# Router on unnormalized rows, and output tiles finished in two halves, in a hybrid attention and MoE layer

## What is computed

```
x1    = x + ga * (mixed @ w_out)                # ga, a2, b2: one value per channel
h2    = x1 * rsqrt(mean(x1*x1) + EPS) * a2 + b2 # a2 = gain * (1 + scale), b2 = shift
score = sigmoid(h2 @ w_router)                  # 16 experts
...                                             # choose 2 experts of one group per token
out   = x1 + gm * sum over chosen experts of weight * expert(h2)
```

## Time and profile before

| | us |
|---|---|
| median of 3 runs | 2009.48 (2003.45 to 2012.72) |
| profiled execution | 2009.4 |
| its span in the trace | 2007.7 |
| output stage, first output matmul to L1408 | 1389.1 to 1504.6 |
| routing, L1408 to the first expert product | 1504.6 to 1553.8 |

### The profile page before, as it was taken

The page is one execution under the profiler, slowest core; times in us unless marked ns, Lnnn a source line. Parts: engine busy times, 40 slices in busy tenths (PEclk is TensorE's granted clock), DMA queues, the critical chain, the costliest instruction groups (busy, mean ns, idle before and its releaser), DMA issues. The chain is left out here.

```text
span 2007.7 us, 22379 instructions
## 1 busy us (share of the span) xinstructions
PE 1817.4 (91%) x8125; PEld 1254.0 (62%) x8125; DVE 933.4 (46%) x1517; ACT 664.2 (33%) x1151; POOL 364.3 (18%) x315
## 2 busy tenths in 40 slices
PE   1999999989898989989989978899983999999996
PEld 1555654555555555655656656687873888888885
DVE  5554313232333342434333436477547464648475
ACT  1421101223232333423324325434212353537373
POOL 3211140000010100101102001100001243436344
PEclk9999998999999999999989988799995999999998
DMA  9334321201110010110000010174334586979694
GB/s 340 137 126 147 85 42 34 63 30 40 37 42 26 22 37 27 29 30 22 27 21 23 15 32 1 63 265 175 126 129 164 168 298 205 305 223 381 202 360 131
DMA packets 121395, 232.38 MB, mean 116 GB/s; under 512 B 5832, under 2 KB 44816, under 8 KB 120240
## 3 DMA queue, kind: packets, MB, share of 16 engines
q1 hardware_dynamic: 113312, 203.14, 29.0%
q0 software_dynamic: 7984, 27.93, 5.7%
HBM read 196.97 MB, written 35.13 MB: 116 GB/s over the span
## 5 line engine op out<-in xcount | busy, mean ns | idle before, releaser
L1797 PE MATMUL psum<-arena 128*128 128x512 f32 x768 | 386.7, 639 | 0.5 <-ACT arena L937 0.4
L1279 DVE TENSOR_REDUCE negm<-psum 128x1 f32<-128x640 f32 (+7 forms) x128 | 90.5, 707 | 423.2 <-PE psum L1724 423.2
L1783 PE MATMUL psum<-kv,arena 128*128 128x64 f32 x1464 | 201.6, 283 | 61.9 <-DVE arena L1255 36.7
L1783 PEld LDWEIGHTS psum<-kv,arena 128*128 128x128 f32 x1464 | 192.1, 204 | 69.6 <-issue 38.2
L723 POOL TENSOR_SCALAR arena<-arena 128x128 f32<-128x128 f32 (+7 forms) x32 | 76.8, 2401 | 854.9 <-ACT arena L931 854.9
L1797 PEld LDWEIGHTS psum<-arena 128*128 128x128 f32 x768 | 144.6, 204 | 128.0 <-issue 127.7
L908 ACT ACTIVATE arena<-psum,negm 128x640 f32<-128x640 f32 (+7 forms) x128 | 89.6, 700 | 402.1 <-DVE negm L1279 402.0
L1623 PE MATMUL psum<-arena 128*128 128x512 f32 (+2 forms) x512 | 189.0, 522 | 0.0
L1921 PE MATMUL psum<-heads_r,kv_r 128*128 128x512 f32 x384 | 150.7, 393 | 15.2 <-DVE kv_r L1509 15.2
L1722 PE MATMUL psum<-kv,heads 112*128 112x512 f32 (+7 forms) x384 | 150.7, 498 | 9.2 <-ACT arena L931 8.6
L1503 DVE TENSOR_TENSOR arena_r<-arena,heads_r 128x2048 fp32r<-128x2048 f32 x64 | 146.6, 2353 | 15.1 <-ACT heads_r L994 15.1
(11 more groups left out here) (376 smaller groups left out, 2729.1 us busy)
## 6 DMA issues: line engine op xcount, KB each, us to landing
arena<-in_w_exp_gate_dram SPq DMA_DIRECT2D x16, 2048.0 KB, 12.0
arena<-in_w_exp_down_dram SPq DMA_DIRECT2D x16, 2048.0 KB, 12.5
arena<-in_w_exp_up_dram SPq DMA_DIRECT2D x16, 2048.0 KB, 14.1
arena<-in_w_ada_dram SPq DMA_DIRECT2D x7, 2048.0 KB, 15.6
arena<-in_w_in_dram SPq DMA_DIRECT2D x24, 512.0 KB, 4.0
z_dram<-arena SPq DMA_DIRECT2D x48, 256.0 KB, 2.0
arena<-z_dram SPq DMA_DIRECT2D x8, 1536.0 KB, 7.9
bc<-in_w_ada_dram SPq DMA_DIRECT2D x4, 2048.0 KB, 7.8
```

Source lines behind the costliest of these rows:

```text
L1279: dve.tensor_reduce(m1, score_buf(u)[:, 0:w], AX.X, ALU.max, negate=True).then_inc(max_ok, 1)
L1783: mm = pe.matmul(psum[:, bank, c * HD:(c + 1) * HD], pt[:, j * P:(j + 1) * P], v, start=(j == 0), stop=(j == u["nb"] - 1))
L1797: mm = pe.matmul(GATE_BANK, gate_w[t % 3][:, k, :], hT[:, k, hf * BANK:(hf + 1) * BANK], start=(k == 0), stop=(k == NK - 1))
```

## The change

The router no longer reads h2. It reads the transposed `x1`, which has neither root nor scale nor shift. The scale is multiplied into the router's weights once (`wr_a2`). The shift's part, b2 times `wr`, is a row of 16 values that 8 more products make once (`rt_bias`, on PE in pass n = 1). The root is one number per token, so DVE applies it and the shift to the 16 results of each tile (`router_logits`). For that the root of each tile gets its own column of `stp`.

`xn2` is still made, since the experts' tokens are gathered from it, but in DVE's next pass of the loop.

From tile 1 on PE finishes bank 0 (high, then low products) before bank 1, with a signal after each; in tile 0 the order is as before. DVE multiplies and adds each half when it is complete.

Thirteen semaphores of the earlier compression stage are folded into four that count; their waits stay where they are.

```diff
+            dve.wait_ge(wr_in, 32)
+            dve.tensor_tensor(wr_a2[:, :, :], wr[:, :, :], mod_a2.unsqueeze(2).to_broadcast([P, NK, NE]), ALU.mult).then_inc(wr_a2_ok, 1)
+
+            def router_logits(n):
+                dve.wait_ge(rt_full, n + 1)
+                dve.scalar_tensor_tensor(logits[:, n * NE:(n + 1) * NE], psum[:, 6 + n % 2, n * NE:(n + 1) * NE], stp[:, 1 + n:2 + n],
+                                         rt_bias[:, :], ALU.mult, ALU.add).then_inc(rt_read, 1)
+
             for n in range(NT + 1):
                 if n < NT:
-                    dve.wait_ge(out_full, n + 1)
                     dve.wait_ge(xr_in[n % 2], 16 * (n // 2 + 1))
-                    if n:
-                        dve.wait_ge(xn2_ok, n)
                     if n >= 2:
                         dve.wait_ge(x1_out[n % 2], 16 * (n // 2))
-                    t2 = x1[n % 2].rearrange("p (a d) -> p a d", a=2)
-                    own(dve.tensor_tensor(t2, psum[:, 2 * (n % 2):2 * (n % 2) + 2, :],
-                                          ga_bc[:, :].rearrange("p (a d) -> p a d", a=2), ALU.mult))
-                    dve.tensor_tensor(x1[n % 2], x1[n % 2], xr[n % 2], ALU.add).then_inc(x1_ok, 1)
+                    for h in range(2):
+                        hs = slice(h * BANK, (h + 1) * BANK)
+                        dve.wait_ge(out_full, 2 * n + h + 1)
+                        own(dve.tensor_tensor(x1[n % 2][:, hs], psum[:, 2 * (n % 2) + h, :], ga_bc[:, hs], ALU.mult))
+                        ins = dve.tensor_tensor(x1[n % 2][:, hs], x1[n % 2][:, hs], xr[n % 2][:, hs], ALU.add)
+                    ins.then_inc(x1_ok, 1)
                     if n + 2 < NT:
                         mixed_lo(n + 2)
                 if n:
+                    m = n - 1
                     dve.wait_ge(xn2T_full, n)
                     dve.tensor_copy(h2T[:, 0:4, :], psum[:, 4, :].rearrange("p (k t) -> p k t", k=4)).then_inc(h2T_dve, 1)
-                if n < NT:
-                    dve.wait_ge(x1_rstd, n + 1)
-                    if n:
-                        dve.wait_ge(xn2_out, 16 * n)
+                    dve.wait_ge(x1_rstd, n)
+                    dve.wait_ge(x1_ok, n)
+                    if m:
+                        dve.wait_ge(xn2_out, 16 * m)
                     else:
                         dve.wait_ge(mod_rows_act, 1)
-                    own(dve.scalar_tensor_tensor(xn2, x1[n % 2], stp[:, 1:2], a2_bc, ALU.mult, ALU.mult))
+                    own(dve.scalar_tensor_tensor(xn2, x1[m % 2], stp[:, 1 + m:2 + m], a2_bc, ALU.mult, ALU.mult))
                     dve.tensor_tensor(xn2, xn2, b2_bc, ALU.add).then_inc(xn2_ok, 1)
+                if n == 1:
+                    dve.wait_ge(rt_bias_full, 1)
+                    own(dve.tensor_copy(rt_bias[:, :], psum[:, 7, BANK - NE:BANK]))
+                if n >= 2:
+                    router_logits(n - 2)
+            router_logits(NT - 1)
...
             def router(n):
+                if n >= 2:
+                    pe.wait_ge(rt_read, n - 1)
                 for k in range(NK):
-                    mm = pe.matmul(psum[:, 6, n * NE:(n + 1) * NE], h2T[:, k, :], wr[:, k, :],
+                    mm = pe.matmul(psum[:, 6 + n % 2, n * NE:(n + 1) * NE], h2T[:, k, :], wr_a2[:, k, :],
...
+                    out_high(0)
+                    if n:
+                        out_low(0)
+                        out_high(1)
+                    else:
+                        out_high(1)
+                        out_low(0)
+                    out_low(1)
                 if 1 <= n <= NT:
-                    if n >= 2:
+                    if n == 1:
+                        pe.wait_ge(x1_ok, 1)
+                        for k in range(NK):
+                            mm = pe.matmul(psum[:, 7, BANK - NE:BANK], mod_b2[:, k:k + 1].to_broadcast([P, P]), wr[:, k, :],
+                                           start=(k == 0), stop=(k == NK - 1))
+                        mm.then_inc(rt_bias_full, 1)
+                        pe.wait_ge(wr_a2_ok, 1)
+                        pe.wait_ge(mod_rows_act, 1)
+                    else:
                         pe.wait_ge(h2T_act, n - 1)
                         pe.wait_ge(h2T_dve, n - 1)
                         router(n - 2)
-                    pe.wait_ge(xn2_ok, n)
+                    pe.wait_ge(x1_ok, n)
                     for k in range(NK):
-                        ins = pe.transpose(psum[:, 4 + k // 4, (k % 4) * P:(k % 4 + 1) * P], xn2[:, k * P:(k + 1) * P],
+                        ins = pe.transpose(psum[:, 4 + k // 4, (k % 4) * P:(k % 4 + 1) * P], x1[(n - 1) % 2][:, k * P:(k + 1) * P],
```

More of the change, by code:

```diff
@@ L172, in hybrid_trunk @@
             "squared", "reduced", "rstd_ok", "tok_ok", "tokT_full", "tokT_dve", "tokT_act"))
-        blk_ok, hid_full, gelu_e, gelu_in, gelu_ok, gelT_full, hid_ok, kcmp_full, kcmp_sq, kcmp_rstd, kcmp_tok, kcmpT_full, kcmp_ok = (
-            sem(s) for s in ("blk_ok", "hid_full", "gelu_e", "gelu_in", "gelu_ok", "gelT_full", "hid_ok", "kcmp_full", "kcmp_sq",
-                             "kcmp_rstd", "kcmp_tok", "kcmpT_full", "kcmp_ok"))
+        cmp_dve, cmp_act, cmp_pe, kcmp_rstd = (sem(s) for s in ("cmp_dve", "cmp_act", "cmp_pe", "kcmp_rstd"))
+        BLK, GELU_IN, GELU_OK, HID_OK, KCMP_TOK, KCMP_OK = range(1, 7)
+        GELU_E, KCMP_SQ = range(1, 3)
+        HID_FULL, GELT_FULL, KCMP_FULL, KCMPT_FULL = range(1, 5)
         mod2_ok = sem("mod2_ok")
@@ L442, in hybrid_trunk @@
         wr, rbias = sb("wr", [P, NK, NE]), sb("rbias", [P, NE])
+        wr_a2, rt_bias = sb("wr_a2", [P, NK, NE]), sb("rt_bias", [P, NE])
+        wr_a2_ok, rt_bias_full, rt_read = sem("wr_a2_ok"), sem("rt_bias_full"), sem("rt_read")
+        logits = heads[:, 6 * D:6 * D + P]
         N_BLK = 2 * T // P + NE
@@ L744, in _ @@
                 one(pool.tensor_scalar(stp[:, 0:1], st[:, SSX:SSX + 1], 1.0 / D, EPS, ALU.mult, ALU.add))
-                pool.tensor_tensor(stp[:, 1:2], stp[:, 0:1], half[:, 0:1], ALU.pow).then_inc(x1_rstd, 1)
+                pool.tensor_tensor(stp[:, 1 + n:2 + n], stp[:, 0:1], half[:, 0:1], ALU.pow).then_inc(x1_rstd, 1)
             pool.wait_ge(xn2_out, 16 * NT)
@@ L867, in _ @@
                 if cc == 2:
-                    act.wait_ge(gelu_in, 1)
-                    act.activation(tmp_ge, tmp_ge, ACT.Exp, scale=-GELU_C).then_inc(gelu_e, 1)
+                    act.wait_ge(cmp_dve, GELU_IN)
+                    act.activation(tmp_ge, tmp_ge, ACT.Exp, scale=-GELU_C).then_inc(cmp_act, 1)
                 act.wait_ge(acc_full, s + 1)
@@ L983, in _ @@
                                    ACT.Copy).then_inc(h2T_act, 1)
-            act.wait_ge(rt_full, NT)
-            act.activation(route[0], psum[:, 6, 0:P], ACT.Sigmoid).then_inc(score_ok, 1)
+            act.wait_ge(rt_read, NT)
+            act.activation(route[0], logits, ACT.Sigmoid).then_inc(score_ok, 1)
             def expert_weights_hi(e, b_e):
@@ L1004, in _ @@
             act.wait_ge(y_lo_ok, NT)
+            act.wait_ge(score_ok, 1)
             expert_weights_hi(0, None)
@@ L1200, in _ @@
             dve.wait_ge(kcmp_rstd, 1)
[L1201 to L1203 removed]
+            dve.tensor_scalar(sq[0:HD, 64:128], psum[0:HD, 2, 0:HD], stp[0:HD, 16:17], None, ALU.mult).then_inc(cmp_dve, 1)
+            dve.wait_ge(cmp_pe, KCMPT_FULL)
+            dve.tensor_scalar(kcmpT[0:HD, :], psum[0:HD, 2, 0:HD], G_KC[0:HD, :], None, ALU.mult).then_inc(cmp_dve, 1)
             own(dve.memset(sel[:, :], 0.0))
@@ L1863, in _, with out_high @@
                     pe.wait_ge(y_lo_ok, n + 1)
-                    for h in range(2):
+                    bank = [psum[:, 2 * (n % 2) + h, :] for h in range(2)]
+                    def out_high(h):
                         w = wout_hi[h].rearrange("p (k n) -> p k n", k=NK)
@@ L1868, in _, with out_low @@
                                 pe.wait_ge(wout_hi_ok, 2 * h + k // 4 + 1)
-                            pe.matmul(psum[:, 2 * (n % 2) + h, :], y_hi[n % 2][:, k, :], w[:, k, :], start=(k == 0), stop=False)
-                            pe.matmul(psum[:, 2 * (n % 2) + h, :], y_lo[n % 2][:, k, :], w[:, k, :], start=False, stop=False)
-                    for h in range(2):
+                            pe.matmul(bank[h], y_hi[n % 2][:, k, :], w[:, k, :], start=(k == 0), stop=False)
+                            pe.matmul(bank[h], y_lo[n % 2][:, k, :], w[:, k, :], start=False, stop=False)
+                    def out_low(h):
                         w = wout_lo[h].rearrange("p (k n) -> p k n", k=NK)
@@ L1875, in _ @@
                                 pe.wait_ge(wout_lo_ok, 2 * h + k // 4 + 1)
-                            mm = pe.matmul(psum[:, 2 * (n % 2) + h, :], y_hi[n % 2][:, k, :], w[:, k, :], start=False,
-                                           stop=(k == NK - 1))
-                    mm.then_inc(out_full, 1)
-                if 1 <= n <= NT:
-                    if n >= 2:
```

(7 more changed lines are left out.)

52 lines of the change are left out of this document (26 added, 26 removed).

## The result

| | before | after |
|---|---|---|
| median of 20 runs each | 2005.08 us (2002.61 to 2012.72) | 2012.18 us (2009.84 to 2020.04) |
| ratio, 95% interval | | 1.0032 (1.0021 to 1.0043) |
| profiled execution | 2009.4 us | 2013.1 us |
| its span | 2007.7 us | 2011.4 us |

The changed kernel is 0.32% slower: 6.4 us by the ratio, 4.2 to 8.6 by its interval (the ratio weighs all runs and is not the quotient of the two medians, 1.0035). That is within 0.5%, as the likeliest case had it; the forecast was +8.0 us on 2009.4, a ratio of 1.0040. More runs of the kernel before brought its median from 2009.48 down to 2005.08, so most of the distance between 2017.4 and 2012.18 lies in the base and not in the sum: on a base of 2005.08 the forecast is 2013.1.

The account below looks back on a forecast made before the run. PE bounds seven output tiles, then a chain of single steps; a 15.16 us lap through the x load exceeds PE's 13.52, moving the first routing operation from 1504.6 to 1512.6. 2009.4 + 8.0 = 2017.4 us, range 2007 to 2022.

Parts of the forecast that it names:

- the likeliest case: Whole kernel: the late x load moves the end by +8.0 us, to 2017.4; chance 0.58, its own range 2014 to 2020.
- a lap: Output stage: from one xn2 through SP, load, halves and copy to the next, 15.16 us against PE's 13.52.
- the last, without mixed_lo: Output stage, pass 6: no mixed_lo, which takes 3.30 us off and leaves a lap of 11.86 us.
- x(7) landed: Last x load of the output stage: lands at 1497.6, 5.3 us after out(7) could be read.
- first routing operation: L1408 on VectorE, after the output stage: starts at 1512.6 instead of 1504.6, +8.0 us.
- The loop: Output stage: xn2, SP, x load, halves, square, mixed_hi, mixed_lo, copy, next xn2; VectorE falls back 1.6 us with each tile.
- The clock at the end: PE after the last tile: 1.2 GHz from router(6) on, each router 3.56 us, transposes 1.97.
- Rival B: End of the output stage: loop binds but PE's clock is granted through the end, +3.7 us, 2013.1; chance 0.08.
- The shift products: PE, pass n = 1: eight new products of mod_b2 with wr cost 1.70 us, so out(7) starts at 1481.1.
- the expert loads: After the output loop: issued some 13 us later, but hidden, since VectorE wants expert 0 only at 1536.9 + 8.
- Rival A: Output stage: load lands in 4.1 us or less and does not bind, -2.1 to -0.1 us, 2008.3; chance 0.19.
- the folded semaphores: Compression stage: renamed semaphores keep every wait in its place, so they cost nothing and gain nothing.

Follow-up runs that it names:

- early_load: Changed kernel with the next x load released by the square, the last reader of its buffer, instead of xn2: median 2008.25 us, ratio 0.9998 to the kernel before.
- own_pass: Changed kernel with xn2 of each tile made in VectorE's own pass again, load wait untouched: median 2006.19 us, ratio 0.9994 to the kernel before.
- out_ahead: Changed kernel with the write of x1 issued as soon as x1 is done, not behind xn2: median 2009.55 us, ratio 1.0009 to the kernel before.
- load_first: Changed kernel with the x load issued ahead of both writes that xn2 releases: median 2019.51 us, ratio 1.0060 to the kernel before.
- own_pass_both: Changed kernel with xn2 in its own pass again and the eight shift products ahead of the output stage: median 2002.14 us, ratio 0.9974 to the kernel before.
- early_both: Changed kernel with the x load released by the square and the shift products ahead of the stage: median 2003.28 us, ratio 0.9981 to the kernel before.
- out_ahead_load_first: Changed kernel with x1's write issued once x1 is done and the x load ahead of xn2's write: median 2004.94 us, ratio 0.9988 to the kernel before.
- before_late_load: Kernel before with only the x load moved behind the two writes that xn2 releases: median 2018.31 us, ratio 1.0055 to the kernel before.

## Why the prediction was right

Step by step, in us from the start of output tile 1 on PE:

| | forecast | measured |
|---|---|---|
| xn2(0) done | 19.0 | 18.9 |
| x(2) landed | 25.0 | 25.0 |
| a lap | 15.16 | 15.20, 15.26, 15.31, 15.35 |
| the last, without mixed_lo | 11.86 | 11.88 |
| x(7) landed | 97.5 | 97.95 |
| router(6) starts | 102.0 | 102.41 |
| transposes of tile 7 | 105.5 | 105.84 |
| router(7) starts | 108.4 | 108.62 |
| first routing operation | 112.5 | 112.93 |

**What bounds it.** The loop is shown by three cuts at different places (the load in early_load, xn2 in own_pass, the write of x1 in out_ahead) that all give back 7.0 to 7.7 us, and by one kernel that puts the late load into the old code and loses 10.5. The 0.36 by which the sum was short is the lap: the four were 0.48 us longer than 4 x 15.16, with a landing of 5.2 for 5.1. PE's own side was as forecast: out(7) started 81.05 us after tile 1 (81.04), and x(7) landed 5.7 us after VectorE could have read it (5.3).

**The clock at the end** was read rightly for this case: after the 7.59 us gap (forecast about 7) PE was at 1.2 GHz through both routers. Rival B did not come.

**What was hidden** stayed so. The shift products (0.4 at most), the halves (0.1), xn2(6) and xn2(7) beside the routers, and the expert loads: the first was issued 111.8 us after tile 1, 98.5 before, and the routing and the time to the first expert product kept their length.

**Where the text was short.** Rival A, the load on time, was priced at -2.1 to -0.1; early_load and own_pass gave +0.66. The kernel early_load lies 0.76 above the upper edge, in three parts: router(6) starts 3.60 us after tile 7's last product and not 3.3; from there to router(7) it is 5.27 and not at most 4.94 (1503.9 - 3.56 - 1495.4), with router(6) and the transposes partly at 1.2 GHz; and from router(7) to the first routing operation it is 4.32 and not 4.17. And the text named the load as the one transfer of the loop. The write of x1 stands in the same loop, and out_ahead and load_first show that it matters as much as the load: x first costs 3.9 us more, x1's write taken out gives 7.0 back. The forecast needed only the load because the load was the later of the two in the order that was built. Last, it expected nothing from the folded semaphores; that the ratios lie below T in nearly every kernel that has them (see above) leaves this open.

## What to carry to other kernels

When a step moves to a later pass, list every transfer that waits on its signal, and for each what buffer it fills or frees; then add up one lap from the signal back to itself and compare it with the period of the bounding engine. Here VectorE was busy less than half the time and the lap was still 1.7 us longer than the period, tile after tile. Cutting the loop anywhere was enough: let a load wait for the last reader of its buffer, and a write for its own data, not for a later result that happens to be signalled.

Work on the bounding engine costs nothing while something else is late, and its full price or more once this is mended: the 1.70 us of products were worth 0.4 at most in the changed kernel and 3.3 in T of own_pass_both, where 1.60 of the 3.3 came with the clock for a reason that is not shown.

## What the runs showed of the hardware that was not expected

- The same end of the stage ran at different clocks. Router(6), 16 instructions, took 1.93 us (own_pass_both, early_both) or 2.65 to 2.70 (early_load, own_pass, out_ahead_load_first) after the same gap of 0.83 us, 3.09 after 1.12 us (out_ahead), and 3.6 after 1.99 and after 7.59 us.
- The order of three 512 KB transfers on one queue changed when the last of them landed: 6.0 us after the first issue with the load last, 6.65 with the load first. A write by itself took 2.6 us; the load took 4.2 with one write behind it.
- The load of x landed 5.0 to 6.1 us after its issue in kernels whose queue order is the same (5.0 to 5.3 in the kernel after, once 6.1 in before_late_load), and a loop without slack keeps each such excess.
